# Two rounded copies of the tokens in their own order, read by TensorE with a stride of eight, in place of copies laid out chunk by chunk

## What is computed

```python
def hierarchical_moe(x, ...):           # x: 256 tokens x 1024, after rmsnorm
    ...                                 # top-1 of 4 groups, top-2 of its 8 experts: combine
    for g in range(N_GROUPS):
        h = jax.nn.silu(jnp.einsum('nd,edf->nef', xt, w_gate[g])) * jnp.einsum('nd,edf->nef', xt, w_up[g])
        out = out + jnp.einsum('nef,efd->nd', h * combine[:, g, :, None], w_down[g])
    return out.reshape(B, S, D)
```

## Time and profile before

| | |
|---|---|
| median of three runs | 1522.1 us (1521.63, 1522.1, 1524.85) |
| profiled execution | 1525.93 us, span 1523.8 us |
| PE busy | 1257.1 us, 82% of the span |
| DVE busy | 746.7 us, 49% |
| ACT busy | 463.8 us, 30% |
| mean DMA rate | 357 GB/s |

### The profile page before, as it was taken

How to read it: one execution, slowest core, us unless ns; L and a number is a source line. 1 busy time by engine, 2 the same in 40 slices (tenths; PEclk the granted TensorE clock), 3 DMA queues, 4 the chain that set the end, 5 groups by cost and what they waited for, 6 DMA issues and landing times.

```text
span 1523.8 us, 21053 instructions
## 1 busy us (share of the span) xinstructions
PE 1257.1 (82%) x8428; PEld 735.5 (48%) x8428; DVE 746.7 (49%) x1791; ACT 463.8 (30%) x1234; POOL 273.8 (18%) x287
## 2 busy tenths in 40 slices
PE   7999999999999988999999886788755555555566
PEld 7787656655565547977755553255311111111112
DVE  5554212212112116557721786677666666667444
ACT  5833110111011015356632244242323232323223
POOL 0000000000000001001000233444433333433331
PEclk9999999999999999999999999899877877887768
DMA  9538999999999999543471499999999999999996
GB/s 391 200 139 348 426 424 425 423 427 423 425 425 425 426 424 364 202 167 117 161 317 56 156 416 421 421 410 421 421 421 420 421 421 421 421 421 420 422 420 272
DMA packets 64582, 544.08 MB, mean 357 GB/s; under 512 B 6624, under 2 KB 7136, under 8 KB 12640
## 3 DMA queue, kind: packets, MB, share of 16 engines
q1 hardware_dynamic: 26160, 273.85, 43.8%
q0 software_dynamic: 38016, 268.45, 42.6%
q10 hardware_dynamic: 304, 0.39, 0.1%
HBM read 541.62 MB, written 1.05 MB: 356 GB/s over the span
## 4 chain that ended last, share of the span: by engine, by line
PE 43%; DMA 42%; DVE 5%; issue 4%; ACT 4%; POOL 2%; DVEq 0%; POOLq 0%; SPq 0%; ACTq 0%
PE PS L203 41%; DMA AR<-in_uv,CO 28%; DMA AR<-in_w_up 10%; DMA EX<-in_w_up 2%; DMA Wk<-in_w_up 2%; DVE AR L2388 2%; PE PS L213 2%; POOL AR L2617 1%; ACT Wk L2283 0%; POOL AR L2591 0%; ACT SM L2277 0%; ACT Wk L1901 0%; ACT HI L192 0%; DMA CO<-in_const 0%; POOL AR L2614 0%
## 5 line engine op out<-in xcount | busy, mean ns | idle before, releaser
L203 PE MATMUL PS<-AR,Wk 64*64 64x512 f32 (+4 forms) x2104 | 393.9, 717 | 169.9 <-ACT Wk L2283 165.7
L2388 DVE CUSTOM_DVE_ANT_0 AR<-AR,PS 128x1024 f32<-128x1024 f32 x193 | 234.9, 1220 | 165.1 <-DMA AR<-in_uv,CO 163.8
L203 PEld LDWEIGHTS PS<-AR,Wk 64*64 64x64 f32 (+3 forms) x2104 | 110.0, 156 | 403.0 <-ACT Wk L2283 271.2
L2617 POOL DMA_INDIRECT AR<-in_uv,CO x186 | 178.3, 959 | 282.2 <-PE PS L203 242.9
L203 PE MATMUL PS<-AR 128*64 128x256 f32 (+3 forms) x1656 | 194.4, 385 | 9.4 <-DMA AR<-in_w_up 5.3
L203 PEld LDWEIGHTS PS<-AR 128*64 128x64 f32 (+3 forms) x1656 | 122.8, 139 | 87.7 <-issue 20.3
L314 POOL TENSOR_TENSOR ST<-ST 128x2 f32<-128x2 f32 (+3 forms) x14 | 12.8, 915 | 789.2 <-DVE ST L1136 480.8
L2273 ACT ACTIVATE RW<-SM 128x2 f32<-128x2 f32 (+1 forms) x132 | 27.0, 205 | 411.5 <-DVE SM L2388 411.5
L1016 DVE TENSOR_TENSOR AR<-AR,PS 128x256 f32<-128x256 f32 x32 | 13.5, 421 | 195.8 <-ACT AR L873 195.8
L199 DVE TENSOR_TENSOR LO<-AR,HI 128x1024 fp32r<-128x1024 f32 x76 | 90.3, 1230 | 32.1 <-ACT HI L192 32.1
L203 PE MATMUL PS<-Wk,AR 128*128 128x128 f32 (+2 forms) x816 | 97.9, 313 | 2.8 <-DMA Wk<-in_w_up 1.2
(11 more groups left out here) (310 smaller groups left out, 1799.1 us busy)
## 6 DMA issues: line engine op xcount, KB each, us to landing
AR<-in_w_up SPq DMA_DIRECT2D x24, 2048.0 KB, 14.7
AR<-in_w_down SPq DMA_DIRECT2D x24, 2048.0 KB, 14.7
AR<-in_w_gate SPq DMA_DIRECT2D x24, 2048.0 KB, 14.7
AR<-in_w_in SPq DMA_DIRECT2D x14, 2048.0 KB, 9.6
EX<-in_w_gate SPq DMA_DIRECT2D x4, 2048.0 KB, 14.7
Wk<-in_w_up SPq DMA_DIRECT2D x4, 2048.0 KB, 14.9
EX<-in_w_down SPq DMA_DIRECT2D x4, 2048.0 KB, 14.7
Wk<-in_w_gate SPq DMA_DIRECT2D x4, 2048.0 KB, 14.8
```

The costliest lines, as they stand in the source:

```text
L203: return pe.matmul(o, l, r, start=start, stop=stop, skip_group_check=True)
L2388: t = dve.tensor_tensor_reduce(r, r, P(6 if g < 128 else 2, 2), 1.0, 0.0, ALU.mult, ALU.add, DT[:, g:g + 1])
L2617: pool.indirect_dma_start(RING[k], None, uv, bass.IndirectOffsetOnAxis(ap=IDX[:, g:g + 1], axis=0)).then_inc(g_in[k], 16)
```

## The change

The two writes keep the order of H in the tiles XGH and XH: ScalarE and VectorE read and write 1024 elements side by side. The gather matmuls take the 128 features of a chunk from them with a stride of eight elements. The instructions, their number, their order on each engine and their waits stay as they are, and so do the values.

```diff
@@ gather_pe
-                    t = mm(pe, o[:, k, :], halves[n % 2][:, tt, (2 * s + k) * 128:(2 * s + k) * 128 + 128], PG[:, b, tt, :, 0, :], n == 0, n == 3)
+                    t = mm(pe, o[:, k, :], halves[n % 2][:, tt, 2 * s + k::8], PG[:, b, tt, :, 0, :], n == 0, n == 3)
@@ first_gather_pe
-                t = mm(pe, o[:, k, :], halves[n][:, tt, (2 * s + k) * 128:(2 * s + k) * 128 + 128], PG[:, 0, tt, :, 0, :],
+                t = mm(pe, o[:, k, :], halves[n][:, tt, 2 * s + k::8], PG[:, 0, tt, :, 0, :],
                        n + tt + k == 0, n + tt == 2)
@@ experts_act
-                act.activation(halves[0][:, tt, :].rearrange("p (c n) -> p c n", c=8), H[:, tt, :].rearrange("p (n c) -> p c n", c=8),
-                               ACT.Copy, scale=ST[:, tt:tt + 1]).then_inc(*m_act.up(f"xh{tt}"))
+                act.activation(halves[0][:, tt, :], H[:, tt, :], ACT.Copy, scale=ST[:, tt:tt + 1]).then_inc(*m_act.up(f"xh{tt}"))
@@ lows
-                by_chunk = lambda v: v.rearrange("p (c n) -> p c n", c=8)
-                dve.scalar_tensor_tensor(by_chunk(halves[1][:, tt, :]), H[:, tt, :].rearrange("p (n c) -> p c n", c=8), ST[:, tt:tt + 1],
-                                         by_chunk(halves[0][:, tt, :].bitcast(F32)), ALU.mult, ALU.subtract).then_inc(*m_dve.up(f"xl{tt}"))
+                dve.scalar_tensor_tensor(halves[1][:, tt, :], H[:, tt, :], ST[:, tt:tt + 1], halves[0][:, tt, :].bitcast(F32),
+                                         ALU.mult, ALU.subtract).then_inc(*m_dve.up(f"xl{tt}"))
```

## The result

The changed kernel took 1542.92 us (median of four runs, 1542.09 to 1543.62) against 1522.51 us: the ratio is 1.0124, 95% interval 1.0112 to 1.0136. By the medians it is 20.4 us slower, by the ratio 18.9 us (17.1 to 20.7 us), where I had forecast one microsecond less.

The account below looks back on a forecast made before the run. The prediction took the start of the weight stream, set by expert 0, to bound the kernel; quicker writes start expert 0 1.04 us sooner and strided loads cost nothing, so 1522.1 - 1.0 = 1521.1 us, range 1519.3 to 1523.8 us.

Parts of the forecast that it names:

- What bounds the kernel: Loop over experts: the weight stream's start sets its end; an earlier expert 0 moves the stream one for one.
- the stream: Transfers of expert weights, first new load issued at 136.02 us, after expert 0's first matrix; claimed never to pause.
- The writes and the path behind them: Ahead of expert 0: ScalarE's writes to 1149 ns, VectorE's to 1282 ns; expert 0 starts 1.04 us sooner.
- the spare matmuls: TensorE's 14 spare matmuls until 127.31 us, ahead of the first gather; they let 0.48 of 0.90 us through.
- I call the extra cost d per gather and take d = 0: Strided loads of 256 gather matmuls: no extra cost per gather, spacing stays 0.119 us, judged by strided transposes.
- the upper end of 0.112 us: Largest d considered per gather, from ScalarE's strided factor of 1.94: spacing 0.231 us in place of 0.119 us.
- The row that I had set aside as the weaker one: Transposes' load times: strided 187 to 193 ns, plain 138 or 139 ns; outweighed by their nearly unmoved spacing.
- TensorE has 18.2 us of room in the loop: At the loop's end, TensorE's own pace brings expert 31's transposes at 560.8 us, against 578.95 us by transfers.
- the sum: Expert 0 and the weight stream 1.04 us sooner, kept to the end: 1522.1 - 1.0 = 1521.1 us.
- TensorE becomes the bound of the loop: Rival, chance 0.05: strided gather loads at d = 0.112 make TensorE overtake the weight stream in the loop, 1531.2 us.

Follow-up runs that it names:

- e3: The change with the stride only in the 32 gather matmuls ahead of the loop, plain loads in the loop: 1526.78 us, ratio 1.0020.
- e5: Against the kernel before: XGH chunk by chunk with plain loads, XH in H's order with strided loads, 128 of 256 loads strided: 1527.05 us, ratio 1.0017.
- e7: The kernel before with TensorE's branch ahead of expert 20 taken out: 1521.64 us, ratio 0.9986.
- e1: The writes of the change, but gather matmuls load 128 columns side by side again: 1521.98 us, ratio 0.9989 to the kernel before.
- e6: The changed kernel with TensorE's branch ahead of expert 20 taken out: 1536.32 us, ratio 1.0082 to the kernel before.
- the two probes: Gather loads varied by group: first stride, float32 and transposes, 1546.24 us; second moving columns, stationary columns and stride, 1533.28 us; one execution each.

## Why the prediction was wrong

**What bounds the kernel** was read rightly: the start of expert 0 moves the stream one for one (e3), and TensorE had some room (e5, e7).

**The writes and the path behind them** were right in mechanism and size: 1142 and 1278 ns measured for 1149 and 1282 ns, the first gather right behind the spare matmuls, and expert 0 1.05 us sooner in e1 for 1.04 us.

**The step that failed is "I call the extra cost d per gather and take d = 0".** It measured 0.124 us, above even the upper end of 0.112 us. I took the transposes as the nearest row, since stride, size and engine are the same. What the runs showed in its place: a matmul's load goes from 192 to 338 ns with the stride, and the gathers from 0.119 to 0.242 us apart. A transposing load is shorter than a matmul's by itself (140 against 190 ns), and a strided one (188 ns) just about as long as a plain one of a matmul. I read that likeness as "no longer than the one to be replaced". The likeness was between a lengthened short load and a plain long one. The row that I had set aside as the weaker one, 138 against 192 ns, was the true sign that a stride lengthens loads; the spacing of transposes could not show it, as it stays at 0.11 us with either load.

**"TensorE has 18.2 us of room in the loop"** was mis-sized too. I extended the pace of experts 1 to 16 to the end. Expert 20 waits 5.5 us at TensorE's branch (e6), and the three experts without gathers take 13.19 us in the changed kernel, not 12.70 us, since without gathers TensorE waits for ScalarE's copy (0.39 us at 585.32 us in the chain) instead: 1.5 us more. The room was 18.2 - 5.5 - 1.5 = 11.2 us. With the measured sizes the sum closes: expert 0 is 2.5 us late, its own gathers cost 1.0 us, and 27 experts cost 0.99 us each, 26.7 us; less 11.2 us of room that is 19.0 us, and the pair of expert 31 is 19.0 us late. At d = 0.124 us and the room as I had it, the rival would have given 12 us.

**The rival "TensorE becomes the bound of the loop"** is what happened, by its mechanism and at its place. I had given it a chance of 0.05 and 1531.2 us. The rule of the Trainium skill that I put beside it ("Advanced Engine Details and Errata", "SBUF Cachelines"), that a reader that takes a new line of 16 bytes at every element pays for it, spoke for it, and three of four rows in the trace did so as well: ScalarE, VectorE and the length of a transpose's load.

## What to carry to other kernels

Here a float32 operand was read at or near full pace as long as two neighbours in the order of reading shared 16 bytes (the loads of TensorE's matmuls, though not of its transposes, 194 ns for 189 ns; ScalarE's write 1222 ns for 1142 ns); moving a stride from a write that is done once to loads that are done 256 times multiplies its cost. Before a cost is set at zero by the likeness of two rows, compare like with like: the same instruction in the same mode, plain and strided. And the room of an engine that is not the bound is to be measured from end to end, with its one-time waits, since they show in no sum once something else hides them.

## What the runs showed of the hardware

- The load of 128 stationary float32r columns (the two probes, the step of 3 from the second): 189 ns at a step of 1, 194 at 2, 262 at 3, 329 at 4, 336 at 8, 316 at 16 elements; matmuls with 256 moving columns start 0.12, 0.12, 0.176, 0.23, 0.245 and 0.225 us apart. That 16 is quicker than 8 I can't explain.
- Transposes of the same data: loads of 140 ns at a step of 1 and 188 to 212 ns from 2 on, 0.11 to 0.12 us apart throughout. Why their strided loads take little over half of a matmul's is not settled.
- A float32 matmul of 256 moving columns with a plain load ran as two instructions 0.217 us apart, and with a strided load 0.24 us: only 0.02 us more each.
- A write of 128 x 1024 elements that reads with a stride of eight took 2234 ns on ScalarE and 2186 ns on VectorE, one side by side 1142 and 1278 ns.
- A branch on a flag read from memory held TensorE's next expert up by 5.5 us in the changed kernel. Taking it out removed the reading of the flag, the jump and the second copy of the code behind it together; which of them costs the time was not tested.
- The granted clock of TensorE from 16 to 40 us was 0.93 in seven of the profiles and 1.00 in six, on the same work, which is worth 1.5 us.
